# First mixer on one core: small products over four PSUM banks, the concatenation split by token halves, and the last pool products moved into other groups

## The chip, the cores and the metric

The kernel runs on one core of one Trainium2 chip. The metric is the device time of one execution in microseconds (us); the figures of the kernel before are those of three runs and of one profiled execution.

## The reference

Two transformer-like blocks over 1024 tokens of width 1024, in float32. Around the change these lines matter (first block):

```
z = rms_norm(h, norm_mix_g);  proj = z @ w_in            # 1024 -> 512 pool | 512 lru | 512 gate
d = (window means of u_pool over 2, 4, 8, 16 tokens) - u_pool
y_pool = (einsum('bsgc,gcd->bsgd', d, pool_w) + pool_b) * pool_scale      # 4 groups of 128
xb = causal_depthwise_conv(u_lru)                         # width 4
r, i = sigmoid(xb @ gate_a_w + ..), sigmoid(xb @ gate_x_w + ..)           # 8 heads of 64
a = exp(8 r log_sigmoid(lru_L));  b = sqrt(1 - a^2) * i * xb
y_lru = linear_recurrence(a, b) * gelu(u_gate)
h = h + concatenate([y_pool, y_lru]) @ w_out              # 1024 x 1024
```

A squared-relu MLP, a gated projection and a final norm follow; the second block is a gated MLP, a mixer (dilated attention beside an S5 state-space branch with a sigmoid GLU, then one 1024 x 1024 product `w_mix_out_2`) and another gated MLP.

## The kernel before, in words

**Products.** Every large product is made of fp32r operands split in a high and a low part: three matmuls (`products`, lines 126 to 128) for one 128 x 128 by 128 x 512 product. Weights come as a stream of 252 units of 512 KB, alternately into the two halves of `raw`. A unit is usable when ScalarE (ACT) has copied its high part (`make_hi`, L117) and VectorE (DVE) has subtracted it (`make_lo`, L121, semaphore `unit_ready`). The units must be converted in the order of the stream, and the next load into a half of `raw` is issued by SyncE only when the unit in it is ready. No planner orders the work: the order on each engine is that of the code, and semaphores join them.

**First mixer, input.** `pe_mix1` runs 12 units m (lru and gate alternately for j = 0 to 3, then pool 3, 2, 1, 0). Each has two groups of 24 matmuls, one per half of the tokens (512), into PSUM banks 0 to 3 in turn (`GROUPS1`, numbered g = 0 to 23). ACT empties each group (L408), converts unit m + 4 (`hi1`), and DVE does `lo1(m + 4)`.

**Small products.** After units 2, 4, 6 and 8, `gates(j)` (L322) makes four products of `XB` with a 128 x 128 gate matrix; the operands are plain f32, and each product appears as two matmul records, which I call passes. After units 9, 10 and 11 `poolmm(0)` to `poolmm(2)`, and at the end `poolmm(3)`, make two products each (L329), of `W2` with `pool_w`. All small products share two banks, 4 and 5, used alternately (`small_bank`). ACT empties those of `gates` (L372, `sig_done`), DVE those of `poolmm` (`pool_out`, L456, `pool_evac`). `lru_act` goes on with exponential, tanh and square root, `recur` (L498 to L509) and `convolve` (L466, L468) run on DVE, and `window_means(i)` (L485 to L492, `d_ready`) makes W2 on DVE after `lo1(m + 4)` of its unit.

**Concatenation.** When all 24 groups are done (`in_done` 24), ACT copies the eight 1024-token channel tiles of `ystage` into A as high parts (L417, order `CAT_ORDER` = 4, 5, 6, 7, 3, 2, 1, 0), and DVE, after `pool_out(3)`, makes the eight low parts (L532, `cat_lo`).

**Output product.** `wide_pe` computes y @ w_out with tokens as rows. Its first half of the columns, six token tiles t = 0 to 5 into banks 0 to 5, runs with k outermost: k tile i of `CAT_ORDER` waits for `cat_lo` i + 1 and for its weights (units 12 to 15, two k tiles each), then 18 matmuls. The other ten groups of 24 matmuls follow one by one.

**Second mixer, its end.** The stream holds the two GLU units and then the eight units of `w_mix_out_2`. ACT and DVE convert the GLU units at the end of `att_act` and `att_dve`, and the first unit of `w_mix_out_2` inside `glu_act` and `glu_dve`, ahead of the second split of heads on DVE (`split_heads_dve`, L1685). `mixo_pe` starts its k loop with that unit and the first split of heads.

Of the kernel before, what the change touches and what calls it, by code (L numbers as in the profile page):

```python
# [44 lines left out]
def program(nc, x, p, stream, cols, rows, gate_mats, pool_mats, inv_count, ssm_g, ssm_bc, x_mid, ssm_mid, att_mid, out):  # L45
# [7 lines left out]
    with ctx:  # L53
# [247 lines left out]
        def tall_group(pe, Z, slot, kd, half, bank, each=None):  # L301
# [7 lines left out]
            return last  # L309

        def pe_mix1(pe):
            def small_bank(q):
# [5 lines left out]
            def gates(j):  # L318
                pe.wait_ge(xb_ready, j + 1)
                for kind in range(2):  # L320
                    for half in range(2):
                        nc.tensor.matmul(ps[:, small_bank(4 * j + 2 * kind + half), :], gate_w[:, 4 * kind + j, :],  # L322
                                         XB[:, half * HALF:(half + 1) * HALF], start=True,
                                         stop=True).then_inc(gates_done, 1)

            def poolmm(i):
                pe.wait_ge(d_ready, i + 1)
                for half in range(2):
                    nc.tensor.matmul(ps[:, small_bank(16 + 2 * i + half), :], pool_w[:, 3 - i, :],  # L329
                                     W2[:, half * HALF:(half + 1) * HALF], start=True,  # L330
                                     stop=True).then_inc(poolmm_done, 1)
# [34 lines left out]
        def lru_act(act, j):  # L366

            for kind in range(2):
                for half in range(2):
                    n = 4 * j + 2 * kind + half  # L370
                    act.wait_ge(gates_done, n + 1)
                    nc.scalar.activation((R, I)[kind][:, half * HALF:(half + 1) * HALF], ps[:, 4 + n % 2, :],  # L372
                                         ACT.Sigmoid, bias=c_(("gate_a_b", "gate_x_b")[kind], j)).then_inc(sig_done, 1)

            if j == 0:
                act.wait_ge(cpos_ready, 3)
            act.wait_ge(sig_done, 4 * j + 4)
            nc.scalar.activation(AA, R, ACT.Exp, scale=c_neg[:, j:j + 1]).then_inc(ex_done, 1)
            nc.scalar.activation(T, R, ACT.Tanh, scale=c_pos[:, j:j + 1]).then_inc(th_done, 1)

            act.wait_ge(q_ready, j + 1)
            nc.scalar.activation(T, Q, ACT.Sqrt).then_inc(sq_done, 1)

        def act_mix1(act):
# [11 lines left out]
            for m, (kind, j) in enumerate(UNITS1):  # L396
# [8 lines left out]
                for half in range(2):  # L405
                    g = GROUPS1.index((m, half))
                    act.wait_ge(in_done, g + 1)
                    nc.scalar.activation(dst[:, half * HALF:(half + 1) * HALF], ps[:, g % 4, :],  # L408
                                         ACT.Gelu_apprx_tanh if kind == "gate" else ACT.Copy
                                         ).then_inc(out_of(m, half)[0], 1)  # L410
                hi1(act, m + 4)
                if m % 2 == 0 and 2 <= m <= 8:
                    lru_act(act, m // 2 - 1)
            for k in CAT_ORDER:
                act.wait_ge(*((y_ready, k - 3) if k >= 4 else (pool_evac, 8 - 2 * k)))
                act.wait_ge(in_done, 2 * TALL1)
                nc.scalar.activation(A[:, k, 0, :], Y[:, k, :], ACT.Copy).then_inc(cat_hi, 1)  # L417

        CAT_ORDER = (4, 5, 6, 7, 3, 2, 1, 0)

        def dve_mix1(dve):
# [31 lines left out]
            def pool_out(i):  # L453
                for half in range(2):
                    dve.wait_ge(poolmm_done, 2 * i + half + 1)
                    nc.vector.tensor_scalar(Y[:, 3 - i, half * HALF:(half + 1) * HALF], ps[:, 4 + half, :],  # L456
                                            c_("pool_b", 3 - i), c_("pool_scale", 3 - i), ALU.add,
# [56 lines left out]
            for m, (kind, j) in enumerate(UNITS1):  # L514
                if m == 0:
                    convolve(0)
                lo1(m + 4)
                if kind == "lru" and j:
                    recur(j - 1)
                    convolve(j)  # L520
                if kind == "pool":
                    if m == 8:
                        dve.wait_ge(mats_in, 48)
                    window_means(m - 8)
                    if m == 8:
                        recur(3)
                    else:
# [16 lines left out]

        def wide_pe(pe, W, ready, norm, order=tuple(range(KD)), banks=6):
            def part(half, t, i, first, last):
# [6 lines left out]

            for i in range(KD):
                ready(i)
                pe.wait_ge(unit_ready, W.n0 + order[i] // 2 + 1)
                for t in range(banks):
                    ins = part(0, t, i, i == 0, i == KD - 1)
                    if i == KD - 1:
                        ins.then_inc(W.done, 1)  # L560
            for g in range(banks, 2 * NT):
# [522 lines left out]
        U_U = U_V + 4  # L1084
        U_GLU = U_U + 4
        U_MIXO = U_GLU + 2
        U_FFN2 = U_MIXO + 8
# [490 lines left out]
        gl_done, gl_s, gl_p, gl_hi, gl_lo = (sem(s) for s in ("gl_done", "gl_s", "gl_p", "gl_hi", "gl_lo"))  # L1578

        def glu_unit(u):  # L1580
            return U_GLU + u, glu_w[:, u], (at_s, NA)

# [28 lines left out]
        def mixo_pe(pe):  # L1611
# [8 lines left out]
            for k in range(4):  # L1620
                pe.wait_ge(unit_ready, U_MIXO + k // 2 + 1)
                pe.wait_ge(ot_lo, k + 1)
# [6 lines left out]
            for k in range(4, KD):  # L1629
                pe.wait_ge(unit_ready, U_MIXO + k // 2 + 1)  # L1630
                pe.wait_ge(gl_lo, 2 * k - 6)
# [21 lines left out]
        def glu_act(act):  # L1653
            split_heads_act(act, 0)
            for q in range(8):
# [195 lines left out]
        def att_act(act):  # L1851
# [31 lines left out]
        def att_dve(dve):  # L1883
# [19 lines left out]
            for n in range(NA):  # L1903
# [371 lines left out]
        def _(pe):  # L2275
            pe.wait_ge(ident_made, 2)
            norm_pe(pe, n_first, 0)
            pe_mix1(pe)
            wide_pe(pe, w_out, lambda i: pe.wait_ge(cat_lo, i + 1), n_mlp, CAT_ORDER)
            step = lambda N, d: lambda: norm_pe_step(pe, N, 0, d)  # L2280
# [11 lines left out]
def pack(i):  # L2292
# [31 lines left out]
    def gated(w):  # L2324
# [4 lines left out]
    w_mix = f("w_mix_in_2")[0]  # L2329
    glu = f("w_glu_2")[0].reshape(4, P, 2, 2, P).transpose(2, 1, 3, 0, 4).reshape(2, P, UNIT)  # L2330
    w_in = tall(f("w_in")[0])
    gate = wide(f("w_ple_gate")[0])
# [62 lines left out]
```

## Time and profile before

| | |
|---|---|
| median of 3 runs | 3134.87 us (3134.37 to 3136.69) |
| the profiled execution | 3137.65 us, of which the span is 3135.8 us |
| PE (TensorE matmul) busy | 3038.2 us, 97% |
| DVE busy | 1356.4 us, 43% |
| ACT busy | 868.7 us, 28% |
| POOL busy | 411.5 us, 13% |
| DMA | 206.98 MB, mean 66 GB/s |

A busy time is a sum over the span; matmuls overlap, and their ends are modelled, so in the rows below the distance from start to start is what counts. A merged row ("x4") gives the start of its first instruction and the time to the end of its last.

### The profile page before, as it was taken

To read this page: it belongs to the slowest core of one execution; us is meant where nothing else is said; L and a number is where in the kernel's file an instruction comes from. 1 tells how busy PE (TensorE), PEld (TensorE's weight loads), DVE (VectorE), ACT (ScalarE), POOL (GpSimd) and SP (SyncE) were. 2 spreads that over 40 slices of the span, in tenths; PEclk is the share of its full clock that TensorE was granted. 3 is DMA by queue.
4 is the path that set the end of the run, shared out by engine and by line. 5 is a ranking of instruction groups with operands and counts; after the bars stand their busy time and mean duration, and the time that the engine had idled before them with its cause. 6 is when DMAs were issued, how large, how long until landed. Compare 5 with 4: busy or idle time off the path is not lost.

```text
span 3135.8 us, 36731 instructions
## 1 busy us (share of the span) xinstructions
PE 3038.2 (97%) x14144; PEld 2486.1 (79%) x14144; DVE 1356.4 (43%) x1755; ACT 868.7 (28%) x1313; POOL 411.5 (13%) x1004
## 2 busy tenths in 40 slices
PE   7999999999999989999999999999898999999998
PEld 5767888888887768888888877887687888888887
DVE  5663444444445353333343353346645333333335
ACT  5523211222114252111111143136644211111112
POOL 0001000000000000788870010012100000000000
PEclk9999999999999999999999999999999999999999
DMA  3112111111112022122221132212122111111113
GB/s 125 41 61 81 61 38 50 54 54 47 38 50 67 27 75 67 66 78 89 96 98 40 41 134 74 82 61 73 61 101 95 61 41 47 47 60 47 40 47 128
DMA packets 54409, 206.98 MB, mean 66 GB/s; under 512 B 7216, under 2 KB 7984, under 8 KB 52000
## 3 DMA queue, kind: packets, MB, share of 16 engines
q1 hardware_dynamic: 38592, 140.53, 13.3%
q0 software_dynamic: 15712, 65.02, 5.6%
q8 instruction: 70, 1.15, 0.1%
q14 instruction: 35, 0.29, 0.0%
HBM read 173.15 MB, written 31.20 MB: 65 GB/s over the span
## 4 chain that ended last, share of the span: by engine, by line
PE 93%; DVE 3%; ACT 2%; issue 1%; DMA 0%; SPq 0%; ACTq 0%; DVEq 0%
PE ps L126 29%; PE ps L128 29%; PE ps L127 29%; PE ps L262 1%; PE ps L1786 1%; PE ps L1812 1%; PE ps L1827 1%; DVE sco L1800 0%; ACT region_b L117 0%; PE ps L1471 0%; ACT junk L198 0%; DVE region_b L121 0%; DVE yb L1438 0%; PE ps L322 0%; DVE region_a L221 0%
## 5 line engine op out<-in xcount | busy, mean ns | idle before, releaser
L126 PE MATMUL ps<-region_a,region_b 128*128 128x512 f32 x1664 | 659.7, 396 | 19.3 <-DVE region_a L221 8.9
L128 PE MATMUL ps<-region_a,region_b 128*128 128x512 f32 x1664 | 651.7, 392 | 0.0
L127 PE MATMUL ps<-region_a,region_b 128*128 128x512 f32 x1664 | 651.2, 391 | 0.0
L126 PE MATMUL ps<-region_b,region_a 128*128 128x512 f32 x1088 | 432.3, 397 | 15.4 <-DVE region_b L121 6.6
L128 PE MATMUL ps<-region_b,region_a 128*128 128x512 f32 x1088 | 428.2, 394 | 0.0
L127 PE MATMUL ps<-region_b,region_a 128*128 128x512 f32 x1088 | 428.0, 393 | 0.0
L818 DVE TENSOR_TENSOR acc<-acc,ps 128x1024 f32<-128x1024 f32 x240 | 292.7, 1220 | 293.8 <-PE ps L128 293.8
L121 DVE TENSOR_TENSOR region_b<-raw,region_b 128x1024 fp32r<-128x1024 f32 x176 | 216.9, 1248 | 401.5 <-ACT region_b L117 401.1
L126 PEld LDWEIGHTS ps<-region_a,region_b 128*128 128x128 f32 x1664 | 315.2, 189 | 87.5 <-DVE region_b L121 8.0
L127 PEld LDWEIGHTS ps<-region_a,region_b 128*128 128x128 f32 x1664 | 315.3, 189 | 65.3 <-issue 1.7
L128 PEld LDWEIGHTS ps<-region_a,region_b 128*128 128x128 f32 x1664 | 314.5, 189 | 66.1
L126 PE MATMUL ps<-region_b 128*128 128x512 f32 x896 | 350.4, 391 | 0.9 <-DVE acc L818 0.9
L128 PE MATMUL ps<-region_b 128*128 128x512 f32 x896 | 348.8, 389 | 0.0
L127 PE MATMUL ps<-region_b 128*128 128x512 f32 x896 | 348.6, 389 | 0.0
L126 PEld LDWEIGHTS ps<-region_b,region_a 128*128 128x128 f32 x1088 | 215.5, 198 | 58.7 <-issue 8.6
L128 PEld LDWEIGHTS ps<-region_b,region_a 128*128 128x128 f32 x1088 | 215.1, 198 | 41.0
L127 PEld LDWEIGHTS ps<-region_b,region_a 128*128 128x128 f32 x1088 | 215.5, 198 | 39.6
L729 ACT ACTIVATE rtmp<-ps 128x512 f32<-128x512 f32 x88 | 52.7, 599 | 628.3 <-PE ps L128 628.3
L117 ACT ACTIVATE region_b<-raw 128x1024 fp32r<-128x1024 f32 x176 | 181.5, 1050 | 159.4 <-DMA raw<-stream 129.7
L121 DVE TENSOR_TENSOR region_a<-raw,region_a 128x1024 fp32r<-128x1024 f32 x74 | 89.5, 1224 | 257.3 <-ACT region_a L117 257.3
L126 PEld LDWEIGHTS ps<-region_b 128*128 128x128 f32 x896 | 168.2, 188 | 35.9 <-DVE acc L818 1.5
L128 PEld LDWEIGHTS ps<-region_b 128*128 128x128 f32 x896 | 168.2, 188 | 35.1
(291 smaller groups left out, 3263.8 us busy)
## 6 DMA issues: line engine op xcount, KB each, us to landing
raw<-stream SPq DMA_DIRECT2D x252, 512.0 KB, 3.3
ssm_row<-ssm_mid POOLq DMA_DIRECT2D x8, 1632.0 KB, 7.4
x_mid<-acc POOLq DMA_DIRECT2D x24, 512.0 KB, 3.1
ssm_mid<-made_osc POOLq DMA_DIRECT2D x8, 1024.0 KB, 4.4
ssm_mid<-made_out POOLq DMA_DIRECT2D x8, 608.0 KB, 3.3
acc<-x SPq DMA_DIRECT2D x8, 512.0 KB, 8.2
rold<-x POOLq DMA_DIRECT2D x16, 256.0 KB, 3.6
old_a<-x_mid POOLq DMA_DIRECT2D x8, 512.0 KB, 8.9
```

What stands on the lines that cost most here:

```text
L117: nc.scalar.activation(slot[:, 0, :], raw[:, odd, :], ACT.Copy).then_inc(hi_done, 1)
L121: nc.vector.tensor_tensor(slot[:, 1, :], raw[:, odd, :], slot[:, 0, :].bitcast(f32), ALU.subtract).then_inc(unit_ready, 1)
L126: nc.tensor.matmul(psum, lhs(0), rhs(0), start=first, stop=False)
L127: nc.tensor.matmul(psum, lhs(0), rhs(1), start=False, stop=False)
L128: return nc.tensor.matmul(psum, lhs(1), rhs(0), start=False, stop=last)
L262: last = nc.tensor.transpose(ps[:, 6 + d % 2, t * P:(t + 1) * P], xn[:, t, d * P:(d + 1) * P], ident[:, :])
L729: nc.scalar.activation(rtmp[:, half, :], ps[:, up_bank(c, j, half), :], ACT.Silu).then_inc(F.sem["ge"], 1)
L818: nc.vector.tensor_tensor(acc[:, t, :], acc[:, t, :], src, ALU.add).then_inc(F.sem["de"], 1)
L1786: last = nc.tensor.matmul(ps[:, 2 * r + c0 // HALF, 0:w], QK[rows_, h // 2, i * P:(i + 1) * P], QK[rows_, 4 + h // 2, c0:c0 + w], start=Tr ...
L1812: last = nc.tensor.transpose(ps[:, 4 + k // 4, (k % 4) * P:(k % 4 + 1) * P], prob[:, n % 2, k * P:(k + 1) * P], ident[:, :])
L1827: last = nc.tensor.matmul(ps[64 * r:64 * r + 64, 6, 0:P], V[:, k, (h + r) * HEAD_DIM:(h + r + 1) * HEAD_DIM], probT[:, (2 * m + r) % 4, k, ...
```

## The change

In the first mixer the small products use banks 4 to 7 in turn; `poolmm(2)` is issued after group 22 (the first half of the last unit) and `poolmm(3)` inside the output product; the concatenation is made of 16 half tiles (8 channel tiles x 2 token halves), the first four of which are made while the last group runs; the last `lo1` comes after the last `window_means`; the first phase of the output product is split into token tiles 0 to 3 and then 4 and 5. In the second mixer the first unit of `w_mix_out_2` moves ahead of the GLU units in the stream and is converted at attention step n = NA - 4.

```
         def small_bank(pe, q):
-                if q >= 2:
-                    pe.wait_ge(*((sig_done, q - 1) if q - 2 < 16 else (pool_evac, q - 17)))
-                return 4 + q % 2
+            if q >= 4:
+                pe.wait_ge(*((sig_done, q - 3) if q - 4 < 16 else (pool_evac, q - 19)))
+            return 4 + q % 4
...
         def pe_mix1(pe):
...
                     tall_group(pe, A, B[:, mm % 4], KD, half, g % 4, each).then_inc(in_done, 1)
+                    if g == 2 * TALL1 - 2:
+                        poolmm(pe, 2)
...
                 if m % 2 == 0 and 2 <= m <= 8:
-                    gates(m // 2 - 1)
-                if m >= 9:
-                    poolmm(m - 9)
-            poolmm(3)
+                    gates(pe, m // 2 - 1)
+                if m == 9 or m == 10:
+                    poolmm(pe, m - 9)
...
+                    if g == 2 * TALL1 - 2:
+                        for piece in range(4):
+                            cat_act(act, piece)
                 hi1(act, m + 4)
                 if m % 2 == 0 and 2 <= m <= 8:
                     lru_act(act, m // 2 - 1)
-            for k in CAT_ORDER:
-                act.wait_ge(*((y_ready, k - 3) if k >= 4 else (pool_evac, 8 - 2 * k)))
-                act.wait_ge(in_done, 2 * TALL1)
-                nc.scalar.activation(A[:, k, 0, :], Y[:, k, :], ACT.Copy).then_inc(cat_hi, 1)
+            for piece in range(4, 16):
+                cat_act(act, piece)
...
+        CAT_PIECES = [(4, 0), (5, 0), (6, 0), (7, 0), (3, 0), (2, 0), (1, 0), (4, 1), (5, 1), (0, 0), (6, 1), (7, 1),
+                      (3, 1), (2, 1), (1, 1), (0, 1)]
+        def cat_act(act, piece):
+            k, half = CAT_PIECES[piece]
+            cut = slice(half * HALF, (half + 1) * HALF)
+            act.wait_ge(*((y_ready, k - 3) if k >= 4 else (pool_evac, 7 - 2 * k + half)))
+            act.wait_ge(in_done, 2 * TALL1 - 1 + half)
+            nc.scalar.activation(A[:, k, 0, cut], Y[:, k, cut], ACT.Copy).then_inc(cat_hi, 1)
+        def cat_dve(dve, piece):
...
+            dve.wait_ge(cat_hi, piece + 1)
+            nc.vector.tensor_tensor(A[:, k, 1, cut], Y[:, k, cut], A[:, k, 0, cut].bitcast(f32),
+                                    ALU.subtract).then_inc(cat_lo, 1)
...
-                lo1(m + 4)
+                if m < TALL1 - 1:
+                    lo1(m + 4)
...
+                    if m == TALL1 - 1:
+                        pool_out(m - 9)
+                        for piece in range(4):
+                            cat_dve(dve, piece)
                     window_means(m - 8)
...
+            lo1(TALL1 + 3)
+            for piece in range(4, 7):
+                cat_dve(dve, piece)
             pool_out(3)
-            for i, k in enumerate(CAT_ORDER):
-                dve.wait_ge(cat_hi, i + 1)
-                nc.vector.tensor_tensor(A[:, k, 1, :], Y[:, k, :], A[:, k, 0, :].bitcast(f32),
-                                        ALU.subtract).then_inc(cat_lo, 1)
+            for piece in range(7, 16):
+                cat_dve(dve, piece)
...
         def wide_pe(pe, W, norm, order, banks=6):
...
+            for tiles in (range(4), range(4, banks)):
+                if tiles[0]:
+                    pe.wait_ge(pool_evac, 6)
+                for i in range(KD):
+                    pe.wait_ge(*cat_done(order[i], tiles[0] // 4))
+                    pe.wait_ge(unit_ready, W.n0 + order[i] // 2 + 1)
+                    for t in tiles:
+                        if i == 0 and t == 3:
+                            pe.wait_ge(pool_in, 8)
+                        ins = part(0, t, i, i == 0, i == KD - 1)
+                        if i == KD - 1:
+                            ins.then_inc(W.done, 1)
+                    if i == 1 and tiles[0] == 0:
+                        poolmm(pe, 3)
...
         def att_act(act):
...
+                if n == NA - 4:
+                    hi_of(act, front_unit())
...
-                if q == 0 or q == 3:
-                    wide_hi(act, mixo, [q // 3])
+                if q == 3:
+                    wide_hi(act, mixo, [1])
...
             split_heads_dve(dve, 0)
-            wide_lo(dve, mixo, [0])
             split_heads_dve(dve, 1)
...
         def att_dve(dve):
...
+                if n == NA - 4:
+                    lo_of(dve, front_unit())
                 ssm_step_dve(dve, n)
...
-             tall(w_mix[:, :1024]), wide(w_mix[:, 1024:]), glu,
-             wide(f("w_mix_out_2")[0]),
+             tall(w_mix[:, :1024]), wide(w_mix[:, 1024:]), mix_out[:1], glu, mix_out[1:],
```

## Rows read from the trace of the kernel before

**Rows 1.** The page: the chain that ended last, shares by engine.

```profile
PE 93%; DVE 3%; ACT 2%; issue 1%; DMA 0%; SPq 0%; ACTq 0%; DVEq 0%
```

**Rows 2.** Waits of PE from 0 to 260 us: us in total, times, longest.

```profile
PE ps L322 <- ACT sc L372: 7.7, 4, 1.9
```

**Rows 3.** Windows of 20 us: busy time by engine, PEclk, DMA share, GB/s.

```profile
200.00:220.00 20.00, 17.96 (x72) 14.40 (x72) 14.61 (x13) 5.07 (x5) 2.12 (x4) 0.86 0.39 129
220.00:240.00 20.00, 20.00 (x90) 16.57 (x89) 4.03 (x6) 0.00 (x0) 2.93 (x6) 1.00 0.25 83
```

**Rows 4.** Timeline of PE, the fourth gates block: start, us, engine, line, operation.

```profile
148.04 1.88 PE L322 MATMUL ps<-sc,gate_w 128*128 128x512 f32 x4
151.83 1.98 PE L322 MATMUL ps<-sc,gate_w 128*128 128x512 f32 x4 [1.92 <-ACT sc L372]
...
153.88 0.39 PE L127 MATMUL ps<-region_a,region_b 128*128 128x512 f32 x1
```

**Rows 5.** Timeline of PE, the first gates block.

```profile
64.12 1.88 PE L322 MATMUL ps<-sc,gate_w 128*128 128x512 f32 x4
67.92 2.83 PE L322 MATMUL ps<-sc,gate_w 128*128 128x512 f32 x4 [1.92 <-ACT sc L372]
...
72.25 0.44 PE L127 MATMUL ps<-region_a,region_b 128*128 128x512 f32 x1
```

**Rows 6.** Timeline of PE, the pool products and the output product's start.

```profile
164.58 1.88 PE L329 MATMUL ps<-scx,pool_w 128*128 128x512 f32 x4
...
166.52 0.40 PE L127 MATMUL ps<-region_a,region_b 128*128 128x512 f32 x1
...
189.87 1.88 PE L329 MATMUL ps<-scx,pool_w 128*128 128x512 f32 x4
...
196.71 3.75 PE L329 MATMUL ps<-scx,pool_w 128*128 128x512 f32 x4 [4.96 <-DVE ystage L456]
...
202.49 0.79 PE L126 MATMUL ps<-region_b,region_a 128*128 128x512 f32 x1 [2.04 <-DVE region_a L532]
...
205.56 0.40 PE L127 MATMUL ps<-region_b,region_a 128*128 128x512 f32 x1
```

**Rows 7.** Timeline of DVE, first mixer.

```profile
138.99 3.92 DVE L468 SCALAR_TENSOR_TENSOR sc<-sc,col 128x1023 f32<-128x1023 f32 x3
...
175.00 0.17 DVE L492 TENSOR_TENSOR scx<-small_f,scx 128x8 f32<-128x8 f32 x1
...
179.00 1.23 DVE L121 TENSOR_TENSOR region_b<-raw,region_b 128x1024 fp32r<-128x1024 f32 x1 [2.38 <-ACT region_b L117]
...
184.50 0.16 DVE L492 TENSOR_TENSOR scx<-small_f,scx 128x4 f32<-128x4 f32 x1
...
192.78 0.15 DVE L485 COPY scx<-scx 128x1 f32<-128x1 f32 x1
...
195.68 0.16 DVE L492 TENSOR_TENSOR scx<-small_f,scx 128x2 f32<-128x2 f32 x1
195.76 1.52 DVE L456 TENSOR_SCALAR ystage<-ps,col 128x512 f32<-128x512 f32 x2
...
201.22 9.16 DVE L532 TENSOR_TENSOR region_a<-ystage,region_a 128x1024 fp32r<-128x1024 f32 x8
```

**Rows 8.** Timeline of ACT, first mixer.

```profile
177.42 0.60 ACT L408 ACTIVATE scx<-ps 128x512 f32<-128x512 f32 x1 [1.62 <-PE ps L128]
...
191.51 6.86 ACT L417 ACTIVATE region_a<-ystage 128x1024 fp32r<-128x1024 f32 x7
```

**Rows 9.** Timeline, end of attention and start of `mixo_pe`, PE and DVE.

```profile
2259.08 0.66 PE L1827 MATMUL ps<-probT,v 128*64 128x128 f32 x8 [2.41 <-DVE att_o L1899]
...
2259.66 1.23 DVE L121 TENSOR_TENSOR glu_w<-raw,glu_w 128x1024 fp32r<-128x1024 f32 x1
...
2269.66 1.22 DVE L1685 TENSOR_TENSOR region_b<-att_o,region_b 128x1024 fp32r<-128x1024 f32 x1
...
2272.66 0.50 PE L126 MATMUL ps<-region_a,region_b 128*128 128x512 f32 x1 [3.33 <-DVE region_a L121]
```

More of the change, by code:

```diff
@@ L309, in tall_group, with small_bank, gates, poolmm @@
             return last
-        def pe_mix1(pe):
-            def small_bank(q):
-                if q >= 2:
-                    pe.wait_ge(*((sig_done, q - 1) if q - 2 < 16 else (pool_evac, q - 17)))
-                return 4 + q % 2
[L318 to L331, printed above, removed]
+        def small_bank(pe, q):
+            if q >= 4:
+                pe.wait_ge(*((sig_done, q - 3) if q - 4 < 16 else (pool_evac, q - 19)))
+            return 4 + q % 4
+        def gates(pe, j):
+            pe.wait_ge(xb_ready, j + 1)
+            for kind in range(2):
+                for half in range(2):
+                    nc.tensor.matmul(ps[:, small_bank(pe, 4 * j + 2 * kind + half), :], gate_w[:, 4 * kind + j, :],
+                                     XB[:, half * HALF:(half + 1) * HALF], start=True,
+                                     stop=True).then_inc(gates_done, 1)
+        def poolmm(pe, i):
+            pe.wait_ge(d_ready, i + 1)
+            for half in range(2):
+                nc.tensor.matmul(ps[:, small_bank(pe, 16 + 2 * i + half), :], pool_w[:, 3 - i, :],
+                                 W2[:, half * HALF:(half + 1) * HALF], start=True,
+                                 stop=True).then_inc(poolmm_done, 1)
+        def pe_mix1(pe):
             for m in range(TALL1):
@@ L371, in lru_act @@
                     act.wait_ge(gates_done, n + 1)
-                    nc.scalar.activation((R, I)[kind][:, half * HALF:(half + 1) * HALF], ps[:, 4 + n % 2, :],
+                    nc.scalar.activation((R, I)[kind][:, half * HALF:(half + 1) * HALF], ps[:, 4 + n % 4, :],
                                          ACT.Sigmoid, bias=c_(("gate_a_b", "gate_x_b")[kind], j)).then_inc(sig_done, 1)
@@ L413, in act_mix1, with cat_done @@
                     lru_act(act, m // 2 - 1)
-            for k in CAT_ORDER:
-                act.wait_ge(*((y_ready, k - 3) if k >= 4 else (pool_evac, 8 - 2 * k)))
-                act.wait_ge(in_done, 2 * TALL1)
-                nc.scalar.activation(A[:, k, 0, :], Y[:, k, :], ACT.Copy).then_inc(cat_hi, 1)
+            for piece in range(4, 16):
+                cat_act(act, piece)
         CAT_ORDER = (4, 5, 6, 7, 3, 2, 1, 0)
+        CAT_PIECES = [(4, 0), (5, 0), (6, 0), (7, 0), (3, 0), (2, 0), (1, 0), (4, 1), (5, 1), (0, 0), (6, 1), (7, 1),
+                      (3, 1), (2, 1), (1, 1), (0, 1)]
+        def cat_done(k, half):
+            return cat_lo, CAT_PIECES.index((k, half)) + 1
+        def cat_act(act, piece):
[5 more added lines that the diff above has]
+        def cat_dve(dve, piece):
+            k, half = CAT_PIECES[piece]
+            cut = slice(half * HALF, (half + 1) * HALF)
+            dve.wait_ge(cat_hi, piece + 1)
+            nc.vector.tensor_tensor(A[:, k, 1, cut], Y[:, k, cut], A[:, k, 0, cut].bitcast(f32),
+                                    ALU.subtract).then_inc(cat_lo, 1)
         def dve_mix1(dve):
@@ L455, in pool_out @@
                     dve.wait_ge(poolmm_done, 2 * i + half + 1)
-                    nc.vector.tensor_scalar(Y[:, 3 - i, half * HALF:(half + 1) * HALF], ps[:, 4 + half, :],
+                    nc.vector.tensor_scalar(Y[:, 3 - i, half * HALF:(half + 1) * HALF], ps[:, 4 + (2 * i + half) % 4, :],
                                             c_("pool_b", 3 - i), c_("pool_scale", 3 - i), ALU.add,
@@ L526, in dve_mix1 @@
                         recur(3)
-                    else:
+                    elif m < TALL1 - 1:
                         pool_out(m - 9)
+            lo1(TALL1 + 3)
+            for piece in range(4, 7):
+                cat_dve(dve, piece)
             pool_out(3)
-            for i, k in enumerate(CAT_ORDER):
-                dve.wait_ge(cat_hi, i + 1)
-                nc.vector.tensor_tensor(A[:, k, 1, :], Y[:, k, :], A[:, k, 0, :].bitcast(f32),
-                                        ALU.subtract).then_inc(cat_lo, 1)
+            for piece in range(7, 16):
+                cat_dve(dve, piece)
         small_f = at("small_f", OFF_ID + 1024 + 512, [16])
@@ L543, in __init__, with wide_pe @@
                 self.n0, self.before, self.evac_of = first_unit, before, evac_of
-        def wide_pe(pe, W, ready, norm, order=tuple(range(KD)), banks=6):
+        def wide_pe(pe, W, norm, order, banks=6):
             def part(half, t, i, first, last):
@@ L551, in part @@
                                 lambda h: slot[:, h, (k % 2) * HALF:(k % 2 + 1) * HALF], first, last)
[L554 to L560, printed above, removed]
+            for tiles in (range(4), range(4, banks)):
[12 more added lines that the diff above has]
+                        poolmm(pe, 3)
             for g in range(banks, 2 * NT):
@@ L1084, in program @@
         U_U = U_V + 4
-        U_GLU = U_U + 4
-        U_MIXO = U_GLU + 2
+        U_FRONT = U_U + 4
+        U_GLU = U_FRONT + 1
+        U_MIXO = U_GLU + 1
         U_FFN2 = U_MIXO + 8
@@ L1578, in program, with front_unit, mixo_unit @@
         gl_done, gl_s, gl_p, gl_hi, gl_lo = (sem(s) for s in ("gl_done", "gl_s", "gl_p", "gl_hi", "gl_lo"))
+        def front_unit():
+            return U_FRONT, A[:, 0], (at_m, NA - NT)
+        def mixo_unit(u):
+            return U_MIXO + u if u else U_FRONT
         def glu_unit(u):
@@ L1620, in mixo_pe @@
             for k in range(4):
-                pe.wait_ge(unit_ready, U_MIXO + k // 2 + 1)
+                pe.wait_ge(unit_ready, mixo_unit(k // 2) + 1)
                 pe.wait_ge(ot_lo, k + 1)
@@ L1629, in mixo_pe @@
             for k in range(4, KD):
-                pe.wait_ge(unit_ready, U_MIXO + k // 2 + 1)
+                pe.wait_ge(unit_ready, mixo_unit(k // 2) + 1)
                 pe.wait_ge(gl_lo, 2 * k - 6)
@@ L2278, in _ @@
             pe_mix1(pe)
-            wide_pe(pe, w_out, lambda i: pe.wait_ge(cat_lo, i + 1), n_mlp, CAT_ORDER)
+            wide_pe(pe, w_out, n_mlp, CAT_ORDER)
             step = lambda N, d: lambda: norm_pe_step(pe, N, 0, d)
@@ L2330, in pack @@
     glu = f("w_glu_2")[0].reshape(4, P, 2, 2, P).transpose(2, 1, 3, 0, 4).reshape(2, P, UNIT)
+    mix_out = wide(f("w_mix_out_2")[0])
     w_in = tall(f("w_in")[0])
```

## The prediction

> **What bounds the kernel now.** I read the chain of waits first: 93% of it is PE, so time is won only where PE stands idle or runs slow [rows 1]. Then the waits of PE in the first 260 us, of which four, 7.7 us in all, stand before gate products [rows 2]; the timeline has 4.96 us more before a pool product and 2.04 us before the output product [rows 6]. The window table shows where the granted clock was not full: 0.86 from 200 to 220 us, and 1.00 right after it with PE busy throughout [rows 3]. Last the timelines, for what each wait consists of. The clock's levels are 2.4 and 1.2 GHz. Units of work on PE, from start to start: four passes and one fp32r matmul take 1.94 us (164.58 to 166.52), and from there to 189.87 lie 95 matmuls and four passes, 23.35 us; so a matmul takes 0.228 us and a pass 0.428 us [rows 6].
>
> The sum is made against the profiled execution, 3137.65 us. The median of the three runs is 2.78 us below it, and I take that off at the end.
>
> **Part 1, four banks for the gates.** A gates block issues four passes, stands 1.92 us until the first sigmoid has emptied its bank, and issues four more: 5.84 us from 148.04 to 153.88, one fp32r matmul included [rows 4]. With four banks nothing in the block waits: 8 x 0.428 + 0.23 = 3.65 us, so 2.19 us saved in each of four blocks, **8.8 us**. What could be late next is `xb_ready`: `convolve(3)` ends at 142.91, and the gates product that needs it comes 5.1 us later [rows 4, 7]. PE will come 2.2 us sooner in each cycle, and the sigmoids end no later than now, so at least 2.9 us of cover stay.
>
> The first block is longer than the others: from 64.12 to the matmul at 72.25 are 8.13 us [rows 5], for work that takes 5.84 + 3 x 0.228 = 6.52 us in the fourth. The excess of 1.61 us lies behind the same wait of 1.92 us, in passes and matmuls at the lower clock. Without the wait I take it as given back, **1.6 us**; bounds 0 and 1.6. The Trainium skill (TensorE: Matmul & The Clock Gate, What's actually happening) says that the monitor behind the gate runs freely, so that one kernel shows different numbers of slow matmuls from run to run. By that rule a slow spell follows the phase as much as the wait, and this term could as well be nothing.
>
> **Part 2, the pool products and the first phase of the output product.** Now, from 189.87 to the matmul at 205.56 are 15.69 us, in which PE issues eight passes and seven matmuls, at full rate 8 x 0.428 + 7 x 0.228 = 5.02 us [rows 6]. The loss is 10.67 us: 4.96 us until `pool_out(2)` has emptied a bank, 2.04 us for `pool_out(3)` and the first L532, the rest slow clock. After the change `poolmm(3)` stands behind two k tiles of the output product, whose operands (token half 0 of tiles 4 and 5) are made during the last group. What can be late, in today's time less the 2.19 us of the fourth gates block:
> - `poolmm(1)` would issue at 177.22 - 2.19 = 175.03 (177.22 is 189.87 less 48 matmuls and four passes). Its W2 is ready at 175.17, and the DVE chain behind it starts at the gates, so it does not move [rows 7]. Wait 0.15 us.
> - `poolmm(2)` comes 4 x 0.428 + 24 x 0.228 = 7.18 us after that, at 182.4. Its W2 hangs on the emptying of group 21, the conversion of unit 14 and the window means: today 177.42 to 184.66 [rows 7, 8]. ACT must first empty group 20 (it may from 175.17, 0.60 us), so group 21 starts at 175.75 and W2 is ready at 183.0. Wait 0.6 us.
> - PE then makes four passes and 24 matmuls, until 190.2, and goes straight into the output product. Four half pieces on ACT (0.60 us each by the L408 row) and on DVE (0.76 us by the L456 row) are done by about 189 [rows 7, 8]. Bank 3 is empty at about 191, while t = 3 of the first k tile is reached nine matmuls in, at 192.3.
> - DVE makes the last window means from about 191.1 to 194.2 (they take 192.78 to 195.84 today, 3.1 us [rows 7]). `poolmm(3)` issues after 24 matmuls, at 195.7: covered by 1.5 us.
> - Unit 15 is converted behind these means, ready at 195.4. The third k tile needs it at 190.2 + 24 x 0.228 + 1.7 = 197.4: covered by 2.0 us, the thinnest cover that costs something when gone.
> - Pieces 4 to 6, `pool_out(3)` and piece 9 are ready by 202, and the eighth k tile comes at 211. The second token half follows 21.9 us of matmuls, with pieces ready by 206.
>
> So of the 10.67 us about 0.8 stay as new waits, **9.9 us** saved. Bounds: 6 (unit 15 late by 4 us, which would be more than all that DVE does behind the means) and 10.7.
>
> **The split in 16 pieces** costs engine time beside PE. Eight whole tiles take 9.16 us on DVE and 0.98 us each on ACT; halves at 0.76 and 0.60 us make 12.2 and 9.6 us [rows 7, 8]. That is 3.0 us more on DVE and 1.8 on ACT, hidden by the 5 to 9 us of cover named above; uncovered it would be that much. The Trainium skill (VectorE: DVE Perf Modes, The TRN2 errata) speaks against it: an operation from SBUF pays a fixed latency each time, so many small tiles pay it many times. The rows agree (half the elements, more than half the time), and by this rule alone the change would lose some us here; the timeline says that PE does not wait for them. The moves of PE waits into `wide_pe` cost nothing that any row shows. POOL's loads of `rold` wait for `poolmm` 8 and come earlier than today. The weight loads 17 to 19 start a few us later relative to PE, needed 45 us on. I take 0.
>
> **Part 3, the second mixer.** Today PE stands 3.33 us until unit 0 of `w_mix_out_2` is split, and starts at 2272.66; after the change it needs only the first split of heads, L1685, ready at 2270.88, so 2270.95: 1.7 us gained [rows 9]. In return the DVE conversion of that unit (1.14 us apart in a queue, by L532's 9.16 / 8) sits at step 60 of attention. DVE has no idle time there, and PE already waits 2.41 us for `finish(29)` at 2259.08 [rows 9]. This wait grows by 1.1 us, and everything to the end of attention moves with it. The copy on ACT fills idle time before it waits for PE. Net **0.5 us** saved; bounds -1.7 (the insertion costs twice its length and more) and +2.9 (the spell of low clock at 2274 goes too).
>
> Sum: 8.8 + 1.6 + 9.9 + 0.5 = 20.8 us. 3137.65 - 20.8 - 2.8 = **3114.1 us**.
>
> **The rivals.**
> - *The slow clock comes back elsewhere.* For it: three equal waits of 1.92 us had no slow spell behind them and one had [rows 4, 5]. Against: the long waits of Part 2 go. Price: the 1.6 us of Part 1 and one more spell of the same size, 3117.3 us.
> - *The third k tile waits for unit 15.* It has moved behind the window means and, with ACT in order, behind the emptying of group 23. If its cover of 2.0 us is short by 5 (today's wait before L329 is 4.96), 3119.1 us. Against: each step is a row of known length.
> - *Attention pays more than `mixo_pe` gains.* 2.2 us worse, 3116.3 us, if the insertion also holds up the scores.
> - *PE catches up with the recurrence.* If `xb_ready` or the weights follow PE's old pace, the gates' gain of three cycles is lost: 3 x 2.19 = 6.6 us, 3120.7 us. Against it the 5.1 us of cover.
> - *The change does not do what it says*: some other semaphore keeps the second pair of gate products and `poolmm(3)` where they are, 3135 us. The waits in the code speak against it.
> - *Slower.* The place is the output product, with the new short waits of 0.15 and 0.6 us and a denser PE ahead of it. If the clock fell to 1.2 GHz there and stayed, each matmul would take 0.428 instead of 0.228 us; 20.8 us are gone after 104 matmuls, 44 us of PE time, and from there the kernel is slower; over all 384 matmuls of the output product (16 groups of 24) it would be 77 us, 3191 us. Against: PE busy without a break kept 1.00 in the window from 220 us [rows 3].
>
> **How the numbers follow.** A measurement here tells about 0.2%, 6.3 us, from no change. Chances: forecast 0.66, clock 0.12, attention 0.08, unit 15 0.07, recurrence 0.04, no effect 0.02, slower 0.01. All but the last two are faster by over 0.2%: faster 0.97, same 0.02, slower 0.01. The range takes in the terms' bounds as they may fall together: down to 3110.5 (upper bounds of Parts 2 and 3), up to 3121 (the recurrence, or unit 15 with some clock loss).
>
> **What would show it.** Right: no wait of L322 for ACT; no gap before L329 above 1 us; about 20 us less from the first gates block to the third k tile; L126 after attention waits for L1685 and not L121; a wait of about 3.5 us before L1827. Wrong in Part 1, if PE waits at L322 for DVE L468; in Part 2, if L126 waits for L121 or for a cat piece; in Part 3, if the wait before L1827 is unchanged. A total above 3125 us would mean that the chain, not PE, set these stages.

## The result, and the profile after

The changed kernel takes 3116.53 us (median of 4, 3112.70 to 3118.67) against 3135.53 us of the kernel before in the same comparison: ratio 0.9937, 95% interval 0.9921 to 0.9953, so 19.8 us less by the ratio (14.7 to 24.8); the medians lie 19.0 us apart. The profiled execution is 3117.56 us with a span of 3115.7 us, 20.1 us below the span of before.

The gates blocks in the timeline of PE of the changed kernel, the first and the fourth (against [rows 4, 5]):

```profile
64.13 3.59 PE L321 MATMUL ps<-sc,gate_w 128*128 128x512 f32 x8
...
67.79 0.40 PE L127 MATMUL ps<-region_a,region_b 128*128 128x512 f32 x1
...
139.75 3.59 PE L321 MATMUL ps<-sc,gate_w 128*128 128x512 f32 x8
...
143.41 0.40 PE L127 MATMUL ps<-region_a,region_b 128*128 128x512 f32 x1
```

Eight passes in one run; from the first pass to the second fp32r matmul 3.66 us in both, where before there were 5.84 in the fourth block and more in the first.

Of the waits of PE from 0 to 260 us (total, times, longest) one row is left that has to do with the small products, in place of 7.7 and 5.0 us [rows 2, 6]:

```profile
PE ps L328 <- DVE scx L516: 0.3, 1, 0.3
```

The timeline of PE around the last three pool products (against [rows 6]), and of DVE in the same stretch (against [rows 7]):

```profile
166.49 0.39 PE L128 MATMUL ps<-region_a,region_b 128*128 128x512 f32 x1
166.93 1.98 PE L328 MATMUL ps<-scx,pool_w 128*128 128x512 f32 x4
...
173.99 0.39 PE L128 MATMUL ps<-region_a,region_b 128*128 128x512 f32 x1
174.68 1.98 PE L328 MATMUL ps<-scx,pool_w 128*128 128x512 f32 x4 [0.31 <-DVE scx L516]
...
187.43 1.88 PE L328 MATMUL ps<-scx,pool_w 128*128 128x512 f32 x4
188.74 0.79 PE L126 MATMUL ps<-region_b,region_a 128*128 128x512 f32 x1
189.37 0.40 PE L127 MATMUL ps<-region_b,region_a 128*128 128x512 f32 x1
```

```profile
174.47 0.16 DVE L516 TENSOR_TENSOR scx<-small_f,scx 128x4 f32<-128x4 f32 x1
174.55 2.97 DVE L480 TENSOR_SCALAR ystage<-ps,col 128x512 f32<-128x512 f32 x4
177.43 2.48 DVE L442 TENSOR_TENSOR region_a<-ystage,region_a 128x512 fp32r<-128x512 f32 x4
182.82 0.15 DVE L509 COPY scx<-scx 128x1 f32<-128x1 f32 x1 [2.90 <-ACT scx L409]
...
185.72 0.16 DVE L516 TENSOR_TENSOR scx<-small_f,scx 128x2 f32<-128x2 f32 x1
185.80 1.22 DVE L121 TENSOR_TENSOR region_b<-raw,region_b 128x1024 fp32r<-128x1024 f32 x1
186.93 1.89 DVE L442 TENSOR_TENSOR region_a<-ystage,region_a 128x512 fp32r<-128x512 f32 x3
188.74 1.52 DVE L480 TENSOR_SCALAR ystage<-ps,col 128x512 f32<-128x512 f32 x2
190.18 5.50 DVE L442 TENSOR_TENSOR region_a<-ystage,region_a 128x512 fp32r<-128x512 f32 x9
```

The means of the last pool group are ready at 185.88, and `poolmm(3)` issues at 187.43, behind 24 matmuls of the output product: nothing waits. From start to start a matmul in a row takes 0.23 us; before `poolmm(1)` it is 0.44 (166.49 to 166.93) and before `poolmm(2)` 0.69, so these two products cost PE 0.2 and 0.5 us of waiting.

For the account by stage I cut both spans at the first gates product, the last addition of the output product, the first scores of attention, the first GLU sigmoid and the last copy of the second output projection. The window rows give length, busy times and, after POOL's, PEclk. Kernel before, then changed kernel:

```profile
64.10:295.70 231.60, 216.19 (x897) 167.14 (x895) 120.59 (x136) 92.27 (x114) 8.99 (x16) 0.97 0.17 55
295.70:2060.60 1764.90, 1733.07 (x7680) 1435.67 (x7680) 739.14 (x835) 418.53 (x612) 347.35 (x879) 0.99 0.19 64
2060.60:2296.50 235.90, 221.62 (x1734) 167.86 (x1734) 136.77 (x366) 139.59 (x264) 38.59 (x75) 0.99 0.21 74
2296.50:2397.40 100.90, 95.25 (x428) 78.25 (x426) 54.88 (x73) 43.39 (x73) 8.00 (x14) 0.98 0.32 115
2397.40:3135.80 738.40, 725.68 (x3200) 599.66 (x3200) 270.00 (x280) 140.10 (x196) 5.55 (x10) 0.99 0.16 57
```

```profile
64.10:275.40 211.30, 210.23 (x897) 165.05 (x895) 120.64 (x143) 91.74 (x122) 8.99 (x16) 1.00 0.18 60
275.40:2040.90 1765.50, 1732.41 (x7682) 1434.76 (x7682) 739.00 (x835) 418.43 (x612) 346.29 (x879) 0.99 0.19 64
2040.90:2274.80 233.90, 220.12 (x1735) 166.52 (x1735) 136.65 (x366) 139.54 (x264) 38.57 (x75) 0.99 0.22 74
2274.80:2376.90 102.10, 96.36 (x428) 79.19 (x426) 54.93 (x74) 43.34 (x73) 7.98 (x14) 0.97 0.31 113
2376.90:3115.70 738.80, 726.14 (x3200) 599.93 (x3200) 269.94 (x280) 140.04 (x196) 5.55 (x10) 0.99 0.17 57
```

The first mixer gave 20.3 us and runs at a full clock with PE busy for 210.2 of 211.3 us. The attention stage gave 2.0 us. Stages that the change does not touch took 0.6, 1.2 and 0.4 us more: 20.3 + 2.0 - 2.2 = 20.1. The granted clock shows where the 1.2 us come from. Before, a spell (a stretch in which the granted clock is half, 1.2 GHz) of 3.4 us lies inside that stage, 100.9 us long; in the changed kernel, 102.1 us, it is one of 6.8 us. The windows, before and then changed, and the whole stage in a kernel that has no spell inside it, "`poolmm(2)` behind the last group" below:

```profile
2379.70:2383.10 3.40, 3.40 (x11) 2.71 (x12) 0.75 (x1) 1.18 (x4) 0.00 (x0) 0.51 0.41 159
```

```profile
2357.00:2363.80 6.80, 5.90 (x18) 4.93 (x19) 2.17 (x4) 2.82 (x5) 0.69 (x1) 0.50 0.19 77
```

```profile
2274.50:2373.80 99.30, 93.65 (x428) 77.01 (x426) 54.87 (x73) 43.38 (x73) 7.99 (x14) 1.00 0.32 117
```

All thirteen profiles follow this, whatever was changed in the mixers: 99.3 to 99.4 us without a spell inside the stage, 100.7 to 101.0 with 3.4 us at the lower clock, 102.1 to 102.2 with 6.8. The long stage before attention behaves alike: 1762.6 to 1763.3 us with 23.9 us at the lower clock in it, 1764.0 to 1765.1 with 27.3 (before: 1764.9), 1765.1 to 1766.3 with 30.7 (changed: 1765.5), 1767.1 with 34.1. For the 0.4 us of the last stage the traces show no cause.

### The profile page after: what moved, and what is told of

It is laid out like the page before. It is cut to its first block, busy times and chain, and to the rows that moved or that the text cites. A ratio compares the mean times of both kernels' runs of the same rounds, so it can differ in the third digit from the quotient of the medians.

```text
span 3115.7 us, 36763 instructions
## 1 busy us (share of the span) xinstructions
PE 3032.7 (97%) x14144; PEld 2483.6 (80%) x14144; DVE 1356.2 (44%) x1763; ACT 867.9 (28%) x1321; POOL 410.4 (13%) x1004
## 4 chain that ended last, share of the span: by engine, by line
PE 94%; DVE 4%; ACT 2%; issue 1%; DMA 0%; ACTq 0%; DVEq 0%
PE ps L126 29%; PE ps L128 29%; PE ps L127 29%; PE ps L262 1%; PE ps L1831 1%; PE ps L1857 1%; PE ps L1872 1%; DVE sco L1845 0%; PE ps L321 0%; ACT junk L198 0%; PE ps L1509 0%; DVE region_b L121 0%; DVE yb L1476 0%; DVE region_a L221 0%; DVE acc L924 0%
## 5 line engine op out<-in xcount | busy, mean ns | idle before, releaser
L117 ACT ACTIVATE region_b<-raw 128x1024 fp32r<-128x1024 f32 x176 | 181.5, 1050 | 145.5 <-DMA raw<-stream 121.5
```

What stands on the lines that cost most here:

```text
L117: nc.scalar.activation(slot[:, 0, :], raw[:, odd, :], ACT.Copy).then_inc(hi_done, 1)
```

## The experiments

The length called **mixer** below is from the first gates product to the last addition of the output product, **attention** from the first scores to the first GLU sigmoid; both come from each run's profile (before 231.6 and 235.9, changed 211.3 and 233.9). The ratios are those of whole kernels against the kernel before.

**Four banks for the gates alone**, in the kernel before:

```
             def small_bank(q):
-                if q >= 2:
-                    pe.wait_ge(*((sig_done, q - 1) if q - 2 < 16 else (pool_evac, q - 17)))
+                if q < 16:
+                    if q >= 4:
+                        pe.wait_ge(sig_done, q - 3)
+                    return 4 + q % 4
+                pe.wait_ge(*((sig_done, q - 1) if q - 2 < 16 else (pool_evac, q - 17)))
                 return 4 + q % 2
...
-                    nc.scalar.activation((R, I)[kind][:, half * HALF:(half + 1) * HALF], ps[:, 4 + n % 2, :],
+                    nc.scalar.activation((R, I)[kind][:, half * HALF:(half + 1) * HALF], ps[:, 4 + n % 4, :],
```

> The kernel before, with four banks for the gate products alone; the pool products keep banks 4 and 5. Theory (each block loses its 1.92 us wait, and PE has cover in the rest): 8.8 us faster than before by the four waits, up to 10.4 if the slow-clock spell behind the first block goes too; each gates block one merged row of 8 passes, 3.43 us. Rival (the recurrence on DVE and ACT sets the pace, so that PE only waits later, at the next xb_ready): 2 to 3 us faster, and a wait of L322 for DVE L468. Rival (what the change wins is only clock): 1 to 2 us.

Measured: 0.9968 (0.9956 to 0.9980), 10.0 us faster; mixer 223.6 us, 8.0 less. No wait is left at the gates, the blocks are single rows as expected (3.59 us, where 3.43 was expected). The slow spell behind the first block is gone; 8.8 + 1.6 would be 10.4. Two things took the rest back. PE comes earlier to `poolmm(1)`; the pool products still have only two banks here, and PE now stands 0.88 us for the emptying of `poolmm(0)` on DVE. And the spell around the last pool product lasts 13.7 us and not 10.2, so the mean clock of the stage stays 0.97. That recurrence and DVE set the pace is refuted at the gates; at the pool products DVE does set it. PE timeline and windows of this kernel, then the window of the kernel before:

```profile
166.97 0.39 PE L128 MATMUL ps<-region_a,region_b 128*128 128x512 f32 x1
168.23 1.96 PE L332 MATMUL ps<-scx,pool_w 128*128 128x512 f32 x4 [0.88 <-DVE ystage L459]
```

```profile
64.60:288.20 223.60, 215.05 (x897) 167.61 (x895) 120.58 (x135) 91.07 (x114) 8.99 (x16) 0.97 0.17 57
186.10:199.80 13.70, 10.00 (x19) 6.13 (x20) 11.25 (x13) 6.24 (x7) 2.12 (x4) 0.50 0.27 95
```

```profile
195.20:205.40 10.20, 6.66 (x11) 3.50 (x12) 7.75 (x10) 6.09 (x7) 2.12 (x4) 0.50 0.31 107
```

**Two banks for the gates again**, in the changed kernel:

```
         def small_bank(pe, q):
-            if q >= 4:
-                pe.wait_ge(*((sig_done, q - 3) if q - 4 < 16 else (pool_evac, q - 19)))
+            if q < 16:
+                if q >= 2:
+                    pe.wait_ge(sig_done, q - 1)
+                return 4 + q % 2
+            pe.wait_ge(*((sig_done, 16) if q < 20 else (pool_evac, q - 19)))
             return 4 + q % 4
...
-                    nc.scalar.activation((R, I)[kind][:, half * HALF:(half + 1) * HALF], ps[:, 4 + n % 4, :],
+                    nc.scalar.activation((R, I)[kind][:, half * HALF:(half + 1) * HALF], ps[:, 4 + n % 2, :],
```

> The changed kernel with two banks for the gate products again, all else as changed. Theory: 8.8 us slower than the changed kernel by the four waits of 1.9 us and their slow first passes, plus 0 to 1.6 us of slow clock, so 10 to 12 us faster than before. If the parts overlap (the waits at the gates had hidden DVE's lateness at the pool products), less than 8 us slower, since the 0.3 us wait at the second pool product would go.

Measured: 0.9960 (0.9946 to 0.9974); mixer 221.3 us, 10.0 more than the changed kernel. The four waits of 1.9 us are back (7.7 in all). This time the slow spell sits behind the third block and not the first. PE timeline of this kernel:

```profile
118.95 1.88 PE L324 MATMUL ps<-sc,gate_w 128*128 128x512 f32 x4
122.75 2.49 PE L324 MATMUL ps<-sc,gate_w 128*128 128x512 f32 x4 [1.92 <-ACT sc L376]
...
126.74 0.63 PE L127 MATMUL ps<-region_a,region_b 128*128 128x512 f32 x1
```

**Three banks for the gates**, in the changed kernel (as above with 3 for 2 and `sig_done` q - 2):

> The changed kernel with three banks in turn for the gate products. Theory: three products issue without a wait, the fourth waits for the first sigmoid: 1.1 to 1.2 us of wait in each block (1.9 with two banks, 0 with four), 4.5 to 5 us more than with four banks from the first gates block to the last addition, plus at most 1.6 us where a slow spell follows. Rival (the conversion of weights and the table load on ACT are what the gates wait for, whatever the banks): the waits stay at 1.9 us.

Measured: 0.9944 (0.9930 to 0.9957); mixer 216.3 us, 5.0 more, with four waits of 1.1 us (4.2 in all) and no slow spell. The waits are 1.9, 1.1 and 0 us for two, three and four banks, as worked out from the sigmoids; by the rival they would have stayed at 1.9.

**Unit 15 first**: `lo1(TALL1 + 3)` ahead of the last `window_means`:

> The changed kernel with unit 15 made ready before the last window means, as in the kernel before, and not after them. Theory: the means end 2.2 us later, at 188.1 us, and poolmm(3) waits 0.5 us for them; 0.5 us slower, the same within the measurement. Rival (the place of that conversion is a main part of the gain): 2 us or more slower.

Measured: 0.9941 (0.9927 to 0.9954); mixer 211.9 us, 0.6 more, and the waits at the pool products 0.7 us instead of 0.3. The order of these two DVE steps is worth about half a microsecond, not 2 or more.

**`poolmm(3)` ahead of the output product**:

```
         def pe_mix1(pe):
...
                 if m == 9 or m == 10:
                     poolmm(pe, m - 9)
+            poolmm(pe, 3)
...
         def wide_pe(pe, W, norm, order, banks=6):
...
-                    if i == 1 and tiles[0] == 0:
-                        poolmm(pe, 3)
```

> The changed kernel with poolmm(3) issued ahead of the output product and not after its second k tile. Theory: PE is there at 182.1 us and W2 at 185.9: a wait of 3.7 us, 3.7 to 5.5 us slower than the changed kernel (the upper end with a spell of slow clock). Rival (the wait of before was for the bank of pool_out(2) alone, which four banks cure): within 1 us of the changed kernel.

Measured: 0.9958 (0.9944 to 0.9972); mixer 217.0 us, 5.7 more. PE timeline of this kernel:

```profile
186.04 3.68 PE L328 MATMUL ps<-scx,pool_w 128*128 128x512 f32 x4 [3.78 <-DVE scx L517]
```

The wait is 3.8 us, and the passes behind it take 3.68 us instead of 1.88: the clock had fallen. So with four banks and an earlier `poolmm(2)`, 3.8 us of the wait of 4.96 us [rows 6] would have stayed.

**`poolmm(2)` behind the last group**:

```
-                    if g == 2 * TALL1 - 2:
+                    if g == 2 * TALL1 - 1:
                         poolmm(pe, 2)
```

> The changed kernel with poolmm(2) issued after the last group (23) and not after group 22; poolmm(3) stays inside the output product. Theory: W2 is free later, so the last window means start about 188.5 instead of 182.8 us and end at 191.6; poolmm(3) would issue at 189.3 and waits 2 to 2.5 us, while the 0.3 us wait before poolmm(2) goes: 1.7 to 2.2 us slower than the changed kernel, 1.5 more if the clock falls behind it. Rival (PE has work enough, the place does not matter): the same time within 0.5 us.

Measured: 0.9940 (0.9926 to 0.9954); mixer 212.5 us, 1.2 more. Less than expected, and by another wait. The timeline of this kernel, PE and DVE:

```profile
182.48 2.49 DVE L442 TENSOR_TENSOR region_a<-ystage,region_a 128x512 fp32r<-128x512 f32 x4
183.22 0.50 PE L126 MATMUL ps<-region_b,region_a 128*128 128x512 f32 x1 [1.50 <-DVE region_a L442]
...
187.78 0.16 DVE L516 TENSOR_TENSOR scx<-small_f,scx 128x2 f32<-128x2 f32 x1
...
188.80 1.88 PE L328 MATMUL ps<-scx,pool_w 128*128 128x512 f32 x4
```

The pieces stand behind `pool_out(2)` on DVE, so the first k tile waits 1.5 us for its piece; in that time the window means catch up, and `poolmm(3)` finds its operand ready. I had placed the wait at the wrong product.

**Whole tiles** instead of halves, the first two before the last window means:

```
-            k, half = CAT_PIECES[piece]
-            cut = slice(half * HALF, (half + 1) * HALF)
+            k, cut = CAT_ORDER[piece], slice(0, S)
...
-            act.wait_ge(in_done, 2 * TALL1 - 1 + half)
+            act.wait_ge(in_done, 2 * TALL1)
```

> The changed kernel with eight whole pieces of the concatenation and not sixteen halves; the first two are made before the last window means, all only after group 23. Theory: PE waits for the emptying of group 23, one whole copy on ACT and one whole subtraction on DVE before its first product: 2.9 us, 2.9 to 4.5 us slower than the changed kernel. Rival (the halves cost DVE and ACT more time in sum, 2 to 3 us, and that shows): the same or faster than the changed kernel.

Measured: 0.9951 (0.9937 to 0.9964); mixer 216.1 us, 4.8 more: the wait of 2.89 us at the output product's first matmul and a spell of slow clock behind it:

```profile
184.52 0.50 PE L126 MATMUL ps<-region_b,region_a 128*128 128x512 f32 x1 [2.89 <-DVE region_a L438]
```

**The second mixer's part alone**, in the kernel before, and **everything but it**:

```
+                if n == NA - 4:
+                    hi_of(act, front_unit())
...
-                if q == 0 or q == 3:
-                    wide_hi(act, mixo, [q // 3])
+                if q == 3:
+                    wide_hi(act, mixo, [1])
...
-             tall(w_mix[:, :1024]), wide(w_mix[:, 1024:]), glu,
-             wide(f("w_mix_out_2")[0]),
+             tall(w_mix[:, :1024]), wide(w_mix[:, 1024:]), mix_out[:1], glu, mix_out[1:],
```

with their DVE halves as in the change; the second kernel has the rest of the change and not these lines.

> The kernel before with the change of the second mixer alone. Theory: between 0 and 2.5 us faster than before: PE waits 1.1 us longer before the products with V at the end of attention and 1.7 us less at the first product of the output projection, and a spell of slow clock after that (1.6 us) goes or stays by its phase. Rival (this part carries a good share of the gain): 5 us or more. Rival (the insertion costs more than it gains): slower than before.

> The changed kernel without the change of the second mixer. Theory: 0 to 2.5 us slower than the changed kernel, so 17.5 to 20.5 us faster than before; PE waits 3.3 us for L121 at the first product of the output projection again.

Measured: alone 0.9998 (0.9989 to 1.0007), attention 233.8 us; all but it 0.9935 (0.9921 to 0.9948), attention 236.6 us. By the whole kernel's time this part cannot be told from nothing. By its stage it gives 2.1 us against the kernel before and 2.7 against the changed kernel without it. In the nine profiles that have it as changed attention is 233.7 to 233.9 us, once 234.9; in the three without it 235.9 to 236.7. PE timeline of the changed kernel (against [rows 9]), then of the kernel without this part:

```profile
2240.60 0.79 PE L1872 MATMUL ps<-probT,v 128*64 128x128 f32 x8 [3.54 <-DVE att_o L1946]
...
2252.51 0.47 PE L126 MATMUL ps<-region_a,region_b 128*128 128x512 f32 x1 [1.70 <-DVE region_b L1731]
```

```profile
2252.67 0.80 PE L126 MATMUL ps<-region_a,region_b 128*128 128x512 f32 x1 [3.33 <-DVE region_a L121]
2253.26 0.63 PE L127 MATMUL ps<-region_a,region_b 128*128 128x512 f32 x1
2253.69 0.63 PE L128 MATMUL ps<-region_a,region_b 128*128 128x512 f32 x1
```

One wait grew by 1.13 us and the other fell by 1.63, both as worked out. Behind the wait of 3.33 us the matmuls follow at 0.43 us from start to start (2253.26 to 2253.69), against 0.23 at the full clock.

**The changed kernel again:**

> The changed kernel once more, for the spread and for the comparison with the kernels beside it. Theory (slow-clock spells fall where the phase puts them): the time from the first gates block to the last addition of the output product is 211 to 212 us again, no slow spell in it, and the time from the first scores to the first GLU sigmoid 233.8 us; the whole kernel between 3112 and 3119 us. Rival (the mixer's gain itself varies from run to run): these two lengths differ by more than 1 us from the first profile's.

Measured: 0.9936 (0.9922 to 0.9949), median 3116.83 us (3115.32 to 3118.79); mixer 211.3 us, attention 233.8. Both stages repeat to 0.1 us, and no slow spell is in the mixer. The two other kernels with this mixer (without the second mixer's part, and the last one below) have 211.3 us as well.

**The DVE half of the front unit behind the loop:**

```
             for n in range(NA):
...
-                if n == NA - 4:
-                    lo_of(dve, front_unit())
...
             inverses(NA // 2 - 1)
+            lo_of(dve, front_unit())
             lo_of(dve, glu_unit(0))
```

> The changed kernel with the subtraction for the first unit of the second output projection moved on DVE from step 60 of attention to behind its loop, where DVE stands idle 4.7 us. Theory: the wait before the products with V falls from 3.5 to 2.4 us and the first product of the output projection still waits for L1731 alone: 1.1 us less from the first scores to the first GLU sigmoid (232.7 us). In the time of the whole kernel this is below what the runs can tell. Rival (the GLU weights then come late, since the next load into that half of raw starts 7 us later): a wait before the first GLU product, the same or slower.

Measured: 0.9919 (0.9905 to 0.9932), median 3112.68 us (3109.93 to 3114.33), beside 3116.83 of the changed kernel in the same comparison; attention 232.7 us. DVE timeline of this kernel:

```profile
2239.43 1.22 DVE L121 TENSOR_TENSOR region_a<-raw,region_a 128x1024 fp32r<-128x1024 f32 x1
2240.57 1.22 DVE L121 TENSOR_TENSOR glu_w<-raw,glu_w 128x1024 fp32r<-128x1024 f32 x1
2245.54 0.29 DVE L1944 COPY rdb<-ps 128x128 f32<-128x128 f32 x1 [3.76 <-PE ps L1877]
```

Both conversions fit in DVE's idle time, the wait before L1872 is 2.41 us again, and 1.1 us are won. The other 3 us between the medians have no such row. In the two profiles the spans are 3112.5 and 3115.0 us: 1.1 of the difference lies in attention and 1.2 in the stage behind it (100.9 and 102.1 us), where this profile has the shorter spell. The two intervals overlap, and what of the 3 us is real stays open. It is the fastest version run, ahead of both kernels.

## Why the prediction was right

The forecast was 3114.1 us; measured were 3116.5 us, which is nearer to the 3117.3 us of the clock rival than to the forecast. The waits that the change removes were read rightly. That the spans agree so well (20.1 us less, 20.8 forecast) is in part luck: attention gave 1.5 us more than its term and the other stages took 2.2 us back. The rest of the 2.4 us is the spread between executions: I took off 2.8 us for the distance of the profiled execution from the median, and in the changed kernel that distance was 1.0. By its parts:

- **Gates, 8.8 us.** The block is 3.66 us where 3.65 was worked out. Undoing it alone cost 10.0 us, with a spell; doing it alone gave 8.0, since part of the gain went into the wait of 0.88 us at `poolmm(1)` and a longer spell. The part is worth its 8.8 us only with more banks for the pool products too. `xb_ready` never became a wait.
- **The spell behind the first block, 1.6 us.** It went, and the mean clock of the mixer rose from 0.97 to 1.00. With two banks in the changed kernel the spell came behind the third block, so the same wait does not bring a spell at the same place in every kernel. The Trainium skill (TensorE: Matmul & The Clock Gate, What's actually happening) says that one kernel shows different numbers of slow matmuls from run to run. The 16 executions of the kernel before agree with that: their mean granted clocks are 0.989 to 0.993, the two slowest (3139.0 and 3139.1 us) at 0.989 and 0.990, the fastest (3131.5 us) at 0.993. The place of this spell did not show it: two profiles with the mixer of before have it behind the first block both times. With the waits gone there was nothing left for a spell to follow. The clock rival failed inside the mixer and held in part outside it, where the other stages took 2.2 us more; 1.8 of these are clock.
- **Pool products and first phase, 9.9 us.** From the first gates product to the 26th matmul of the output product the changed kernel takes 189.37 - 64.13 = 125.2 us. Before, the eighth started at 205.56 and 18 more take 4.1, so 209.7 - 64.1 = 145.5 us for the same work. That is 20.3 measured, and 8.8 + 1.6 + 9.9 = 20.3 expected. The new waits were 0.2 us at `poolmm(1)` and 0.5 at `poolmm(2)`, worked out as 0.15 and 0.6. The cover of `poolmm(3)`, 1.5 us, was 187.43 - 185.88 = 1.55. That of unit 15, 2.0 us, was 1.7: it was ready at 187.02, and the third k tile began at 188.74. The variants put a price on each piece of the part: 4.8 us for the halves, 5.7 for the place of `poolmm(3)`, 1.2 for the place of `poolmm(2)`, 0.6 for the order of unit 15. Each is the loss when that piece alone is missing, so they overlap and do not add up to 9.9. No run has four banks for the pool products and nothing else of the part.
- **The halves' cost.** 16 pieces took 2.48 + 1.89 + 5.50 = 9.9 us on DVE, against 9.16 for eight whole ones, so 0.7 and not 3.0 us more: I had priced them by L456, another operation, which empties a bank and takes 0.76 us apiece in a pair; the subtractions of halves follow each other at 0.61 us. The Trainium skill's rule on many small tiles (VectorE: DVE Perf Modes, The TRN2 errata) has the right sign here, with 0.7 us of DVE time as its number, and no weight, since PE does not wait for them.
- **Second mixer, 0.5 us: mis-sized.** Its two waits moved as worked out (3.54 and 1.70 us). The term left the slow spell behind the first product to the upper bound of 2.9; measured were 2.0 to 2.9 (1.0 against before in the one profile at 234.9 us), since the spell behind the first product went with the shorter wait each time.

What failed is the size of that last term and the silence on the rest: other stages gave 2.2 us back. The first is clock and lies within its bounds; the second is clock for 1.8 us and open for 0.4. The lower end of the range was also added up wrongly: the upper bounds of Parts 2 and 3 give 3114.1 - 0.8 - 2.4 = 3110.9, not 3110.5.

## What to carry to other kernels

Small products that PE issues between large groups can cost the time of their evacuation: four of them made PE wait 1.9, 1.1 and 0 us with two, three and four banks. Count banks against the products of a block, not against engines. Where a serial chain on another engine ends a stage, look for the part of the next stage whose operands are already there (here two k tiles of one token half) and put the late product behind it. A conversion moved forward to take it off one path should be put where its engine idles, one step away from the path it would enter.

## What was not expected of the hardware

Slow spells follow some waits and not others, and the length of the wait tells which only in part. In the gates blocks and the end of attention, 1.2 GHz was granted within 2 us of the end of the wait behind 3.54 us in all nine profiles that had it, behind 3.33 us in all three and behind 2.41 us in all four; behind 1.92 us at the gates it was one block of four, the first in two kernels and the third in another; behind 1.70 us it was none of ten, and behind 1.1 us none of four. The same program spreads over some 8 us between executions, 3131.5 to 3139.1 us in 16 runs of the kernel before, while the mixer without a spell in it took 211.3 us in all four profiles that have it as changed, and the mixer of before 231.6 and 231.7 us in two. An effect of 2 us is read from the length of its stage in a profile, not from the time of the whole.
